# Sample attention of a hybrid decoder step rewritten: page chunks on partitions, query folded into the compression weights

## The reference, cut to what matters

```
k_cmp, v_cmp = compress(page rows)        # blocks of 32 rows, stride 16: sum_j (row_j + pe_j) @ w_j, w_j 64 x 64 -> 255 blocks
s = qc @ k_cmp.T / 8;  p_cmp = softmax;   o_cmp = p_cmp @ v_cmp
imp = p_cmp grouped by selection block of 64 rows, summed over the 4 heads of a kv head;  top 8 of 65 blocks are kept
s = qr @ k_sel.T / 8, blocks not kept masked;  o_sel = softmax(s) @ v_sel
s = qr @ k_win.T / 8 over the last 512 rows;   o_win = softmax(s) @ v_win
o = g0 * o_cmp + g1 * o_sel + g2 * o_win
```

## Time and profile before

| | |
|---|---|
| median of 3 runs | 4165.94 us (4154.78 to 4166.95) |
| profiled execution: span, first to last instruction | 4154.0 us |
| TensorE busy | 3430.4 us (83%) |
| VectorE busy | 1308.6 us (32%) |
| ScalarE busy | 936.8 us (23%) |
| GpSimd busy | 318.0 us (8%) |
| mean granted TensorE clock | 0.908 |
| moved by DMA | 267.52 MB, mean 64 GB/s |

### The profile page before, as it was taken

One profiled execution on the slowest core, in us unless ns is written; L12 is line 12 of the kernel. 1 busy time (PEld: TensorE's weight loads), 2 busy tenths in 40 slices (PEclk: granted clock), 3 DMA queues, 4 the chain that ended last, 5 costly groups with the idle time before them and its releaser, 6 DMA issues. The chain is left out here.

```text
span 4154.0 us, 41676 instructions
## 1 busy us (share of the span) xinstructions
PE 3430.4 (83%) x14220; PEld 2213.5 (53%) x14220; DVE 1308.6 (32%) x2656; ACT 936.8 (23%) x1783; POOL 318.0 (8%) x358
## 2 busy tenths in 40 slices
PE   7887968755689996777878669966798999997999
PEld 4544547654566775444544334444345666664665
DVE  2334645543166563232232112222112333332000
ACT  2342312110033442432334111111111121221000
POOL 1110012210011000100000000000000000000000
PEclk9998988875699998989899789988999999998999
DMA  3111000011200002724332412124222111112120
GB/s 119 57 47 44 25 19 10 10 48 52 50 13 22 24 12 82 209 65 133 101 89 75 175 63 75 66 111 168 89 81 60 30 40 30 40 31 52 49 74 35
DMA packets 256314, 267.52 MB, mean 64 GB/s; under 512 B 72337, under 2 KB 187794, under 8 KB 255826
## 3 DMA queue, kind: packets, MB, share of 16 engines
q1 hardware_dynamic: 255122, 262.08, 20.6%
q10 hardware_dynamic: 1088, 4.20, 0.3%
HBM read 222.39 MB, written 48.04 MB: 65 GB/s over the span
## 5 line engine op out<-in xcount | busy, mean ns | idle before, releaser
L2953 PE MATMUL up_acc<-hnT,up_w 128*128 128x364 f32 (+1 forms) x2112 | 645.4, 469 | 11.0 <-DMA up_w<-in_w_up 11.0
L2953 PEld LDWEIGHTS up_acc<-hnT,up_w 128*128 128x128 f32 x2112 | 402.0, 190 | 254.2 <-issue 12.7
L3054 PE MATMUL down_acc<-mlp_gT,down_w 128*128 128x364 f32 (+1 forms) x1056 | 323.7, 470 | 30.4 <-DMA down_res<-scr_h2T 30.4
L3054 PEld LDWEIGHTS down_acc<-mlp_gT,down_w 128*128 128x128 f32 x1056 | 201.4, 191 | 152.7 <-issue 32.3
L1926 PE MATMUL ns_b<-ns_cT,ns_wab 128*128 128x256 f32 x512 | 240.6, 644 | 27.6 <-ACT ns_cT L1898 22.3
L1898 ACT ACTIVATE ns_cT<-ns_b 64x256 f32<-64x256 f32 x512 | 193.8, 379 | 135.2 <-PE ns_b L1949 128.7
L391 PE MATMUL chan_acc<-xnT,chan_w 128*128 128x364 f32 (+1 forms) x576 | 185.7, 485 | 44.1 <-DMA chan_w<-in_w_in 28.0
L1926 PEld LDWEIGHTS ns_b<-ns_cT,ns_wab 128*128 128x128 f32 x512 | 114.7, 227 | 146.5 <-issue 141.5
L324 PE MATMUL proj_p<-proj_w_nat,proj_xT 128*128 128x512 f32 (+1 forms) x432 | 176.0, 570 | 14.3 <-ACT proj_xT L219 14.3
L391 PEld LDWEIGHTS chan_acc<-xnT,chan_w 128*128 128x128 f32 x576 | 112.7, 197 | 116.9 <-issue 53.8
L2992 DVE TENSOR_SCALAR up_y<-up_xp,up_tap 128x1024 f32<-128x1024 f32 x44 | 35.8, 813 | 423.8 <-ACT up_xs L2964 423.8
(11 more groups left out here) (551 smaller groups left out, 4911.5 us busy)
## 6 DMA issues: line engine op xcount, KB each, us to landing
ns_pg<-in_cache_kv SPq DMA_DIRECT2D x256, 256.0 KB, 2.9
up_w<-in_w_up SPq DMA_DIRECT2D x44, 512.0 KB, 4.5
down_w<-in_w_down SPq DMA_DIRECT2D x8, 1408.0 KB, 6.5
xs_kn<-in_cache_mem SPq DMA_DIRECT2D x8, 1024.0 KB, 6.4
xs_v<-in_cache_mem SPq DMA_DIRECT2D x8, 1024.0 KB, 8.4
...
```

The costliest lines, as they stand in the source:

```text
L2953: m = pe.matmul(acc[n][:, g, 0:b - a], w[:, s, n, k, :], hnT[:, k, a:b], start=(k == 0), stop=(k == KD - 1))
L3054: m = pe.matmul(acc[s][:, g, 0:b - a], w[:, s, f, :], gT[:, f, a:b], start=(f == 0), stop=(f == FT - 1))
```

## The change

All engines' parts of the stage are new, and nothing else but some constant tables. One sequence n is treated at a time, the eight of them written out without loops.

- Pages come by gathers that GpSimd issues: a page is eight chunks of 16 rows, a chunk is 32 KB in one run, and 128 chunks (half h of a sequence) go to 128 partitions in one indirect DMA. X has two slots of two halves; sequence n uses slot n % 2, and its gather waits for pv_done of sequence n - 2.
- The query is multiplied into the 32 key weights once for four sequences (query_weights, on n = 0 to 3 at the head and 4 to 7 within n = 3), giving qw, 16 x 2 x 32 columns for each sequence and kv head. block_scores multiplies qw by the turned k_cmp of the 16 row positions; three matmuls with ident and shift add the two halves of each block. There are no compressed keys any more.
- For the values, the compressed probabilities are multiplied by the raw v_cmp columns of X (into Y), the result is turned (turns 18 and 19) and multiplied by the value weights wv into C. v_cmp is not turned.
- A sequence has 25 turns (turn, up to four transposes each) through three banks A and six buffers tb; DVE empties those of ON_DVE, ACT the others. v_sel is read from X directly (values), with the 64 query rows of half h at output rows 64h.
- Loads, gates and the window copies are all issued on SP; loads of window n + 1 wait for pvw_done of n.

The diff, cut (`...` marks what is left out; the new code is moved left):

```diff
@@ -1694,424 +1694,641 @@
...
-def compress(c):
-    for kv in range(2):
-        for p in range(8):
-            x = pe.matmul(bank[c][:, kv * 256:(kv + 1) * 256], wab[:, c, p, kv, :], cT[:, c, kv, p:PAST // 2:8],
-                          start=(p == 0), stop=(p == 7))
-    return x
...
-                        a = act.activation(cT[HD * q:HD * (q + 1), c, kv, 256 * s:256 * (s + 1)],
-                                           bank[4 * (s % 2) + c][HD * kv:HD * (kv + 1), q:512:2], ACT.Copy)
...
+        X = [st.sb(f"x{s}", [P, 2, NJ, 512]) for s in range(2)]
+        qw = st.sb("qw", [P, 4, NJ, 2, 32])
+        wkT = st.sb("wkT", [P, 2 * NJ, HD])
+        wv = st.sb("wv", [P, 8, 2, HD])
...
+sp.dma_start(idx0[:, :], io["pages"]).then_inc(idx_here, 16)
+sp.dma_start(chunk_no[:, :], io["chunk_no"]).then_inc(idx_here, 16)
...
+w_v = io["cmp_w"].rearrange("c j d e -> c (j d) e").rearrange("c (t p) e -> c p t e", p=P)
+for u in range(2):
+    sp.dma_start(wdup[:, :, u, :], w_v[0]).then_inc(w_here, 16)
...
+for n in range(NB):
+    if n + 1 < NB:
+        sp.wait_ge(pvw_done, n + 1)
+        load_win(n + 1)
+        if n + 2 < NB:
+            load_nv(n + 2)
+    sp.wait_ge(of_ready, n + 1)
+    for kv in range(2):
+        sp.dma_start(scr["mix"][SEQ + n * NT:SEQ + (n + 1) * NT, 256 * kv:256 * (kv + 1)].rearrange("t (g d) -> g t d", g=4),
+                     of[32 * kv:32 * kv + 32, n % 2, :]).then_inc(o_out[n % 2], 16)
...
+rows = io["cache_kv"].rearrange("a (c j) n -> (a c) (j n)", c=8)
+def load(n):
+    for h in range(2):
+        k = 2 * n + h
+        pool.indirect_dma_start(X[n % 2][:, h, :, :].rearrange("p j n -> p (j n)"), None, rows,
+                                bass.IndirectOffsetOnAxis(ap=idx[:, k:k + 1], axis=0)).then_inc(x_here[n % 2][h], 16)
+pool.wait_ge(idx_ready, 1)
+load(0)
+pool.wait_ge(setup_turned, 7)
+load(1)
+for n in range(2, NB):
+    pool.wait_ge(pv_done, n - 1)
+    load(n)
...
+def query_weights(half):
+    qm = [qzc[:, 4 * half:4 * half + 4, v, :, :].rearrange("p n g t -> p n (g t)") for v in range(2)]
+    for p in range(8):
+        if p >= 2:
+            pe.wait_ge(qw_kept_act if p % 2 == 0 else qw_kept_dve, 4 * half + p // 2)
+        elif half:
+            pe.wait_ge(y_kept_act if p == 0 else y_kept_dve, 4)
+        for x in range(4):
+            for v in range(2):
+                m = pe.matmul(Y[p % 2][64 * v:64 * v + 64, x * P:(x + 1) * P].rearrange("p (n q) -> p n q", n=4),
+                              wkT[:, 2 * p + x // 2 + NJ * (x % 2), :], qm[v], start=True, stop=True)
+        m.then_inc(qw_done, 1)
...
+def turn(n, i, srcs):
+    g = group(n, i)
+    if g >= NA:
+        wait_kept(pe, *turn_of(g - NA))
+    for x, src in enumerate(srcs):
+        t = pe.transpose(bank(n, i)[:, x * P:(x + 1) * P], src, ident[:, :])
+    t.then_inc(turned, 1)
+def turn_keys(n, i):
+    if i == 0:
+        for h in range(2):
+            pe.wait_ge(x_here[n % 2][h], 16 * (n // 2 + 1))
+    turn(n, i, [X[n % 2][:, h, j, 0:P] for j in (2 * i, 2 * i + 1) for h in range(2)])
+def turn_selected(n, i, jq, h):
+    turn(n, i, [X[n % 2][:, h, 4 * jq + x, 256:384] for x in range(4)])
+def block_scores(n, pp):
+    if pp == 0:
+        if n == 0:
+            pe.wait_ge(small_kept, 1)
+        else:
+            pe.wait_ge(oc_read, n)
+        if n % 4 == 0:
+            pe.wait_ge(qw_kept_act, n + 4)
+            pe.wait_ge(qw_kept_dve, n + 4)
+    for i in (2 * pp, 2 * pp + 1):
+        wait_kept(pe, n, i)
+        for x in range(2):
+            j = 2 * i + x
+            for v in range(2):
+                r = slice(HD * v, HD * (v + 1))
+                m = pe.matmul(C[r, 0:256], qw[r, n % 4, j, :, :].rearrange("p a q -> p (a q)"),
+                              buf(n, i)[r, x * 256:(x + 1) * 256], start=(j == 0), stop=(j == NJ - 1))
+    if pp == 3:
+        m.then_inc(cs_done, 1)
+def key_scores(n, k, i, jq):
+    m5 = 5 * n + k
+    if m5 >= 2:
+        wait_scores_kept(pe, m5 - 2)
+    wait_kept(pe, n, i)
+    wait_kept(pe, n, i + 1)
+    for h in range(2):
+        m = pe.matmul(SB[m5 % 2][64 * h:64 * h + 64, :], qzr[:, n, :, :, :].rearrange("p v g t -> p (v g t)"), buf(n, i + h)[:, :],
+                      start=True, stop=True)
+    m.then_inc(ss_done, 1)
...
+def values(n, jq):
+    wait_kept(pe, n, 20 + jq)
+    for x in range(4):
+        for h in range(2):
+            j = 4 * jq + x
+            pe.matmul(Y[0][64 * h:64 * h + 64, 0:P], buf(n, 20 + jq)[:, x * P + 64 * h:x * P + 64 * h + 64],
+                      X[n % 2][:, h, j, 384:512], start=(j == 0), stop=(j == NJ - 1 and h == 0), skip_group_check=True)
+def fold_rows(n):
+    pe.wait_ge(rows_ready, n + 1)
+    at = Y[1][0:64, 256:320]
+    pe.matmul(at, fold[:, 0, :], oc[:, :], start=True, stop=False)
+    pe.matmul(at, fold[:, 1, :], os[:, :], start=False, stop=True).then_inc(fold_done, 1)
+for n in range(NB):
+    s = n % 2
+    for i in range(4):
+        turn_keys(n, i)
+    block_scores(n, 0)
+    turn_keys(n, 4)
+    turn_keys(n, 5)
+    block_scores(n, 1)
+    turn_keys(n, 6)
+    turn_keys(n, 7)
+    block_scores(n, 2)
+    turn_selected(n, 8, 0, 0)
+    turn_selected(n, 9, 0, 1)
+    block_scores(n, 3)
+    if n:
+        fold_rows(n - 1)
+    turn_selected(n, 10, 1, 0)
+    turn_selected(n, 11, 1, 1)
+    key_scores(n, 0, 8, 0)
+    pe.wait_ge(sb_ready, n + 1)
+    pe.matmul(C[:, 0:256], ident[:, :], sb[:, 1:257], start=True, stop=False)
+    pe.matmul(C[:, 0:256], shift[:, 0, :], sb[:, 2:258], start=False, stop=False)
+    pe.matmul(C[:, 0:256], shift[:, 1, :], sb[:, 0:256], start=False, stop=True).then_inc(join_done, 1)
+    pe.wait_ge(win_here, 16 * (n + 1))
+    turn(n, 12, [win[:, x, 0:P] for x in range(4)])
+    window_scores(n)
+    turn_selected(n, 13, 2, 0)
+    turn_selected(n, 14, 2, 1)
+    key_scores(n, 2, 10, 1)
+    pe.wait_ge(p_ready, n + 1)
+    pe.matmul(C[:, 0:258], gsum[:, :], pc[:, :], start=True, stop=True).then_inc(gsum_done, 1)
+    turn(n, 15, [pc[:, 0:P], pc[:, P:2 * P]])
+    key_scores(n, 3, 13, 2)
+    turn_selected(n, 16, 3, 0)
+    turn_selected(n, 17, 3, 1)
+    if n:
+        pe.wait_ge(of_ready, n)
+    if n == 0:
+        pe.wait_ge(qw_kept_act, 4)
+        pe.wait_ge(qw_kept_dve, 4)
+        pe.wait_ge(wv_here, 32)
+    wait_kept(pe, n, 15)
+    for jj in range(2):
+        for h in range(2):
+            for v in range(2):
+                m = pe.matmul(Y[jj][64 * v:64 * v + 64, :], buf(n, 15)[:, h * P + 64 * v:h * P + 64 * v + 64],
+                              X[s][:, h, 8 * jj:8 * jj + 8, P + HD * v:P + HD * (v + 1)], start=(h == 0), stop=(h == 1))
+        m.then_inc(y_done, 1)
+    key_scores(n, 4, 16, 3)
+    for k in range(2):
+        pe.wait_ge(y_kept_dve if k else y_kept_act, n + 1)
+        turn(n, 18 + k, [ysb[:, (4 * k + x) * P:(4 * k + x + 1) * P] for x in range(4)])
+    pe.wait_ge(imp_read, n + 1)
+    for k in range(2):
+        wait_kept(pe, n, 18 + k)
+        for x in range(4):
+            for v in range(2):
+                p = 4 * k + x
+                m = pe.matmul(C[64 * v:64 * v + 64, 0:P], buf(n, 18 + k)[:, x * P + 64 * v:x * P + 64 * v + 64],
+                              wv[:, p, :, :].rearrange("p u e -> p (u e)"), start=(p == 0), stop=(p == 7))
+    m.then_inc(oc_done, 1)
+    if n == 3:
+        query_weights(1)
+    def turn_p(jq):
+        pe.wait_ge(exp_done, 5 * n + jq + 1)
+        turn(n, 20 + jq, [S[:, (4 * jq + x) * P:(4 * jq + x + 1) * P] for x in range(4)])
+    if n == 3:
+        pe.wait_ge(qw_kept_act, 8)
+        pe.wait_ge(qw_kept_dve, 8)
+    turn_p(0)
+    turn_p(1)
+    values(n, 0)
+    turn_p(2)
+    values(n, 1)
+    turn_p(3)
+    values(n, 2)
+    pe.wait_ge(exp_done, 5 * n + 5)
+    wait_kept(pe, *turn_of(group(n, 24) - NA))
+    at = bank(n, 24)
+    for x in range(2):
+        pe.transpose(at[:, x * P:(x + 1) * P], S[:, 2048 + x * P:2048 + (x + 1) * P], ident[:, :])
+    for x in range(2):
+        t = pe.transpose(at[0:NT, (2 + x) * P:(3 + x) * P], pn[:, x, :], ident[:, :])
+    t.then_inc(turned, 1)
+    values(n, 3)
+    wait_kept(pe, n, 24)
+    pe.wait_ge(nv_here[s], 32 * (n // 2 + 1))
+    bw = buf(n, 24)
+    pe.matmul(Y[0][64:128, 0:P], bw[0:NT, 256 + 64:256 + 128], nv[:, s, 0, :], start=False, stop=True,
+              skip_group_check=True).then_inc(pv_done, 1)
+    for x in range(2):
+        for h in range(2):
+            pe.matmul(Y[1][64 * h:64 * h + 64, 0:P], bw[:, x * P + 64 * h:x * P + 64 * h + 64], win[:, 2 * h + x, P:2 * P],
+                      start=(x == 0), stop=(x == 1 and h == 0), skip_group_check=True)
+    pe.matmul(Y[1][64:128, 0:P], bw[0:NT, 384 + 64:384 + 128], nv[:, s, 1, :], start=False, stop=True,
+              skip_group_check=True).then_inc(pvw_done, 1)
+fold_rows(NB - 1)
...
+for n in range(NB):
+    for i in (0, 2, 4, 6, 8):
+        evacuate(n, i)
+    act.wait_ge(cs_done, n + 1)
```

(113 more changed lines are left out.)

658 lines of the change are left out of this document (284 added, 374 removed).

## The result

The changed kernel takes 3926.0 us (median) against 4164.9 us: a ratio of 0.943, 95% interval 0.941 to 0.945, 239 us less. Of the four executions behind this median three took 3920.4 to 3926.9 us, and one, in a slower state, 4985.1. The profiled execution took 3920.4 us. The forecast was 3876 us, so the sign was right, the time lies inside the range of 3835 to 4015, and some 50 of the 290 us that were forecast did not come. It lies outside the 3835 to 3920 that the forecast had for itself, and within 4 us of the 3930 of rival 1: by the number alone rival 1 would have been believed, and what follows shows that it is not the cause.

The account below looks back on a forecast made before the run. PE bound the stage, compress dearest at 236 us, not DMA. Head 53, sequences 352, second query_weights 8.5 and tail 7 gave 420.5 us against 710, 290 less: 3876 us, range 3835 to 3920 (4015 with two rivals).

Parts of the forecast that it names:

- rival 1: In block_scores, matmuls in different row halves writing one bank don't overlap: 54 us more, 3930 us; chance 0.16.
- The prices: PE record costs: 0.105 us for 128 columns, 0.21 for 256, 0.42 for 512; a change of work 0.15.
- Half price for alternating column strips: PE records alternating between strips of 64 columns overlap and cost half; full price would add 19.7 us a sequence.
- A sequence by itself: PE time per sequence: 32.4 us work, 4.2 changes, 4.8 waits, 2.1 clock; taken as 44 us against 85.5.
- turn 18's copy: Before the value weights' matmuls, PE waits 2.1 us a sequence for DVE to empty turn 18.
- the 0.94 taken from the turning phase of before: PE's granted clock through a sequence, taken from the old kernel's turning phase; adds 2.1 us a sequence.
- the second query_weights: Query multiplied into key weights for sequences 4 to 7, inside n = 3: adds 8.5 us.
- window n + 1 is wanted 15 us into the next sequence: free: SP's window loads now wait for pvw_done but are needed only 15 us into the next sequence, so cost nothing.
- The head: From the stage's first load to the first key turn, waiting for gathers and weights: 53 us, between 39 and 60.
- the tail: Stage's end after the last sequence: final operations, fold and copy, two stores and barrier, 7 us.
- Rivals 2 to 4: Nothing overlaps, 4013 us, chance 0.11; gather bounds at 125 GB/s, 4079 us, 0.07; gather slower still, 4656 us, 0.05.

Follow-up runs that it names:

- run 2: Changed kernel with the window loaded in 4 KB packets instead of 1 KB, order of issue unchanged: 3856.9 us, ratio 0.928.
- run 1: Changed kernel with GpSimd waiting for the previous window to land before it issues each gather: 3856.5 us, ratio 0.928.
- Run 4: Changed kernel with the gather of sequence 1 issued only after the constants and gates have landed: 3908.8 us, ratio 0.940.
- run 10: Changed kernel with 4 KB window packets, windows ahead of gathers, head loads reordered, window copies one a sequence, turn 18's copy before mask 3: 3826.8 us, ratio 0.920.
- run 6: Changed kernel with 4 KB window packets and nearly all block-score matmuls in one tile, omitting kv head 1's compressed scores: 3927.8 us, ratio 0.943.

## Why the prediction was right, and where it fell short

- **The prices were right.** From start to start, with the forecast in brackets including 0.15 us for the change of work, 16 block-score records take 1.87 us (1.83), four of key scores 1.01 (0.99), 16 by raw value rows 3.48 (3.51), 32 of value weights 1.89 (1.83), 16 of values 1.02 (0.99), eight transposes 1.02 (1.03). Half price for alternating column strips held throughout, and the Y matmuls with runs of 64 columns cost what adjacent ones do.
- **A sequence by itself** was given 44 us and takes 41.3 to 42.7 where no window wait is in it (run 2). In run 2 the waits of PE come to 3.1 us a sequence, not 4.8 (16.2 for turn 18's copy, 6.1 and 2.1, over eight), and from 1733 to 1900 us its clock is 0.99, not the 0.94 taken from the turning phase of before. In all, eight sequences of run 2 with the second query_weights take 342.5 us (301.2 by their starts and the last one 41.4), and 360.5 were forecast: 18.0 too many.
- **The step that failed** is "window n + 1 is wanted 15 us into the next sequence: free". The 15 us were right (the turn comes 16 us in). The landing was put at nothing, as if the load were alone (3.7 us in run 1), though the same text places an 8.4 MB gather at the same moment: both pvw_done and pv_done come at a sequence's end. It cost 65.3 us by the starts of sequences 0 and 7 (366.5 us against 301.2 in run 2), 10.9 in each of six sequences, 8.1 of them waiting and the rest at lower clock.
- **The head**, 53 forecast, range 39 to 60, was 60.8. The sum had the bytes and not the order: small loads that PE wants first stood behind a gather. Run 4 gives 46.5 and run 10 gives 39.8, the bottom of the range.
- These add up: 65.3 - 18.0 + 7.8 and 0.2 for the tail are 55.3 us over the forecast stage, which is what was measured.
- **Luck** has its part in the number. The 18 us too many hid a good quarter of the 65 that were missing. And the range reached to 4015 only for the sake of rivals 1 and 2, of which neither came true; without them it ended at 3920, under the measured time.
- **Rival 1**, that row halves writing one bank don't overlap, is refuted, though its 3930 us is nearer to the measured 3926 than the forecast: 1.94 us for 16 records against 3.67 in one tile, and run 6 puts 6.6 us a sequence on it, where the rival had 6.7. The rule of the Trainium skill, TensorEngine Tiling (Array Packing), Gotcha 1: PSUM Pressure, which spoke for it, doesn't describe these pairs, whose results go to different partitions of the bank; the measurement decides. **Rivals 2 to 4** fall with the lengths above and with gathers at 358 GB/s; no key turn of sequences 1 to 7 waits for X. That the gather might bound was looked at from every side but this one, what else lands late because of it.
